# Experts chosen from a table of pairwise comparisons, and another order of the work around the last tile

## The reference: what is computed

```
h   = rmsnorm(x) * g1;   q,k,v,o,i,f,u = h @ w_in
hm  = mLSTM(q, k, v, i, f)  per head, normed, * sigmoid(o)      # running state C, n, m
x1  = x + [hm | multi-scale trailing means of u @ pool_w] @ w_out
h2  = rmsnorm(x1) * g2
group  = top-1 of 4 groups by softmax(h2 @ w_rg + b_rg)
expert = top-2 of the 4 experts of that group by softmax(h2 @ w_re + b_re)
y   = rmsnorm(x1 + sum over the 2 experts of share * (silu(h2 @ w_gate[e]) * (h2 @ w_up[e])) @ w_down[e]) * g_f
```

## Time and profile before

| what | value |
|---|---|
| median of 3 runs | 938.84 us |
| lowest and highest run | 938.76, 940.09 us |
| profiled execution, span from first to last instruction | 939.7 us |
| mean granted TensorE clock | 0.976 |
| PE busy, share of the span | 880.8 us, 94% |
| DVE, POOL, ACT busy | 431.1, 374.6, 154.5 us |

### The profile page before, as it was taken

One profiled execution on the slowest core, in us unless ns is written; L12 is line 12 of the kernel. 1 busy time (PEld: TensorE's weight loads), 2 busy tenths in 40 slices (PEclk: granted clock), 3 DMA queues, 4 the chain that ended last, 5 costly groups with the idle time before them and its releaser, 6 DMA issues.

```text
span 939.7 us, 16689 instructions
## 1 busy us (share of the span) xinstructions
PE 880.8 (94%) x6339; PEld 755.1 (80%) x6339; DVE 431.1 (46%) x1166; ACT 154.5 (16%) x456; POOL 374.6 (40%) x576
## 2 busy tenths in 40 slices
PE   5989999999999999999989799999999999999960
PEld 3974987869588695886945699999999999999920
DVE  3144474645646456463557843333333333333264
ACT  2031212121311213111131210000000000000071
POOL 4040031210302103021150258767767776777524
PEclk9989999999999999999999899999999999999985
DMA  9930203030110301003027389999999999999883
GB/s 328 280 151 1 68 1 80 12 79 1 28 52 1 79 1 34 25 1 57 1 62 291 71 294 299 327 352 335 360 346 333 327 322 326 315 319 314 248 305 115
DMA packets 90039, 163.15 MB, mean 174 GB/s; under 512 B 48887, under 2 KB 59027, under 8 KB 81770
## 3 DMA queue, kind: packets, MB, share of 16 engines
q1 hardware_dynamic: 70062, 136.43, 41.5%
q0 software_dynamic: 17728, 25.28, 11.2%
q10 hardware_dynamic: 2188, 0.59, 0.3%
HBM read 139.83 MB, written 25.87 MB: 176 GB/s over the span
## 4 chain that ended last, share of the span: by engine, by line
PE 51%; DMA 16%; issue 11%; POOL 11%; DVE 9%; ACT 1%; POOLq 1%; DVEq 0%; SPq 0%; ACTq 0%
PE bank L1527 48%; DMA z_d<-wout,win 12%; POOL z_d L599 7%; DVE wout L1443 2%; POOL wout L551 2%; PE bank L1532 1%; DVE wout L1436 1%; DVE win L1482 1%; DMA wout<-h_d,idt 1%; DMA h2T<-z_d 1%; DVE win L1407 1%; PE bank L1732 0%; DMA xbuf<-in_x_prompt 0%; POOL pad L595 0%; PE bank L1645 0%
## 5 line engine op out<-in xcount | busy, mean ns | idle before, releaser
L1527 PE MATMUL bank<-wout,win 128*128 128x150 f32 (+3 forms) x2048 | 246.3, 282 | 1.1 <-DVE wout L1129 1.1
L1527 PEld LDWEIGHTS bank<-wout,win 128*128 128x128 f32 x2048 | 244.7, 190 | 1.2 <-DVE wout L1129 1.2
L1527 PE MATMUL bank<-hT,win 128*128 128x128 f32 (+1 forms) x1536 | 182.9, 279 | 0.0
L1527 PEld LDWEIGHTS bank<-hT,win 128*128 128x128 f32 x1536 | 178.6, 192 | 1.5 <-issue 1.2
L1527 PE MATMUL bank<-win 128*128 128x130 f32 (+5 forms) x1024 | 137.3, 294 | 2.7 <-DVE win L1428 1.4
L599 POOL DMA_INDIRECT z_d<-wout,win x75 | 125.2, 1669 | 27.1 <-issue 26.8
L1527 PEld LDWEIGHTS bank<-win 128*128 128x128 f32 (+2 forms) x1024 | 125.5, 191 | 12.3 <-issue 10.3
L1527 PE MATMUL bank<-win,hT 128*128 128x260 f32 (+3 forms) x512 | 122.2, 417 | 3.0 <-DVE xbuf L1247 1.5
L1527 PE MATMUL bank<-wout,mixT 128*128 128x512 f32 (+1 forms) x384 | 116.8, 487 | 1.8 <-ACT mixT L845 1.7
L1527 PEld LDWEIGHTS bank<-win,hT 128*128 128x128 f32 (+1 forms) x512 | 77.1, 173 | 43.0 <-issue 34.1
L1436 DVE STREAM_TRANSPOSE wout<-bank 128x480 f32<-128x480 f32 (+1 forms) x45 | 25.1, 603 | 156.7 <-DMA z_d<-wout,win 155.2
(11 more groups left out here) (308 smaller groups left out, 812.0 us busy)
## 6 DMA issues: line engine op xcount, KB each, us to landing
win<-in_w_gate SPq DMA_DIRECT2D x32, 1024.0 KB, 6.3
win<-in_w_up SPq DMA_DIRECT2D x32, 1024.0 KB, 9.2
win<-in_w_down SPq DMA_DIRECT2D x32, 1024.0 KB, 10.6
win<-in_w_in SPq DMA_DIRECT2D x4, 2048.0 KB, 20.1
xbuf<-in_x_prompt SPq DMA_DIRECT2D x8, 512.0 KB, 3.8
wout<-in_w_out SPq DMA_DIRECT2D x1, 4096.0 KB, 15.6
z_d<-xbuf SPq DMA_DIRECT2D x32, 128.0 KB
h_d<-xn SPq DMA_DIRECT2D x8, 512.0 KB, 2.7
```

The costliest lines, as they stand in the source:

```text
L1527: return nc.tensor.matmul(out, lhsT, rhs, start=first, stop=last)
```

## The change

Routing: `routing` makes one table of all "a >= b" pairs of the four group values and of the four expert values in each group (5 x 4 x 4 numbers a token), and finds each number's rank by two sums and a subtraction; the group is the number of the highest rank, the experts those of rank one and two. What the first expert alone, the slots and the shares need is split off into `picks_of`, `gaps` and `shares`.

Order: in round 9 the first part of `mix_start` for tile 8 stands ahead of tile 7's norm, with its last product (`decayed`) behind; the state's update, tile 7's logits copy and two of the five `first_turn` transposes stand inside `head_out`, where DVE waits for ACT; ACT's copies of x1 (`picked_rows`) stand behind the decay matrix and the norm. For tile 8, DVE's routing runs straight on in round 9, PE's transposes start with the first half of x1, `seats` (the slots) of tile 7 stands behind tile 8's routing and that of tile 8 behind `first_rows`, and PE's `state_transposes` stands behind `ranks(8)`.

```diff
             def h2_evac(t):
                 R = ROWS[t]
-                after(dve, "h2T_done", t + 1)
                 after(dve, "lo_done", t)
                 for n in range(2):
+                    after(dve, "h2T_done", 2 * t + n + 1)
                     last = v.tensor_tensor(h2T[:, 4 * n:4 * n + 4, 0:R], bank(h2_bank(t, n), P, 4, R),
                                            wide(g2[:, 4 * n:4 * n + 4], [P, 4, R]), ALU.mult)
...
             def routing(t):
...
+                five = rt[0:R, 0:NR].rearrange("p (g e) -> p g e", e=EPG)
+                cubed = [R, EG + 1, EPG, EPG]
+                ge = duel[0:R]
+                ahead, lost, rank = (wins[0:R, c, :].rearrange("p (g e) -> p g e", e=EPG) for c in range(3))
+                goh = rt[0:R, 32:36]
+                link(v.tensor_tensor(ge, five.unsqueeze(3).broadcast_to(cubed), five.unsqueeze(2).broadcast_to(cubed), ALU.is_ge))
+                link(v.tensor_tensor(ge, ge, below[0:R].unsqueeze(1).broadcast_to(cubed), ALU.mult))
+                link(v.tensor_reduce(out=ahead, in_=ge, axis=AX.X, op=ALU.add))
+                link(v.tensor_reduce(out=lost, in_=ge.rearrange("p g a b -> p g b a"), axis=AX.X, op=ALU.add))
+                link(v.tensor_tensor(rank, lost, ahead, ALU.subtract))
+                link(v.tensor_tensor(goh, rank[:, 0], seat[0:R, 0], ALU.is_equal))
+                two = cube_of(R)
+                link(v.tensor_tensor(two, rank[:, 1:], seat[0:R, 1].unsqueeze(1).broadcast_to([R, EG, EPG]), ALU.is_le))
+                v.tensor_tensor(oh[0:R, t, 2, :].rearrange("p (g e) -> p g e", e=EPG), two, wide(goh, [R, EG, EPG]), ALU.mult
+                                ).then_inc(S["route_ready"], 1)
+                dve.wait_ge(S["route_ready"], t + 1)
+            def cube_of(R):
+                return rt[0:R, 64:64 + NE].rearrange("p (g e) -> p g e", e=EPG)
+            def picks_of(t):
+                R = ROWS[t]
+                one = cube_of(R)
+                rank = wins[0:R, 2, :].rearrange("p (g e) -> p g e", e=EPG)
+                link(v.tensor_tensor(one, rank[:, 1:], seat[0:R, 0].unsqueeze(1).broadcast_to([R, EG, EPG]), ALU.is_equal))
+                link(v.tensor_tensor(oh[0:R, t, 0, :].rearrange("p (g e) -> p g e", e=EPG), one, wide(rt[0:R, 32:36], [R, EG, EPG]),
+                                     ALU.mult))
+                link(v.tensor_tensor(oh[0:R, t, 1, :], oh[0:R, t, 2, :], oh[0:R, t, 0, :], ALU.subtract))
+            def gaps(t):
+                R = ROWS[t]
+                diff = rt[0:R, 64:64 + NE]
+                link(v.tensor_reduce(out=rt[0:R, 56:57], in_=rt[0:R, 0:EG], axis=AX.X, op=ALU.max))
+                v.tensor_tensor(rt[0:R, 20:24], rt[0:R, 0:EG], rt[0:R, 56:57].broadcast_to([R, EG]), ALU.subtract)
+                link(v.tensor_tensor(diff, oh[0:R, t, 1, :], oh[0:R, t, 0, :], ALU.subtract))
+                link(v.tensor_tensor(diff, diff, rt[0:R, EG:NR], ALU.mult))
+                v.tensor_reduce(out=rt[0:R, 29:30], in_=diff, axis=AX.X, op=ALU.add).then_inc(S["rexp_in"], 1)
+            def shares(t):
...
+                else:
+                    seats(t)
+            def seats(t):
+                R, place = ROWS[t], rt[0:ROWS[t], 80:96]
+                if t == LAST - 1:
+                    place = kept[0:R]
...
                 v.tensor_tensor(isb[0:R, :, 0:DH], nsb[0:R, :, 0:DH], wide(den, [R, H, DH]), ALU.mult).then_inc(S["hv_ready"], 1)
                 if t == 1:
                     h_evac(3)
+                if t == LAST:
+                    new_state(LAST)
+                    partial_logits(LAST - 1)
+                    first_turn(range(2, 4))
                 after(dve, "hs0", t + 1)
                 r = newton(R, sm[0:R, 16:20], sm[0:R, 24:28], 28, H, 1.0 / DH)
...
                 if i == NT:
                     mix_start(LAST)
+                    norm_x1(LAST - 1)
+                    decayed(LAST)
                     mix_b(LAST)
                     h2_evac(LAST - 1)
-                    first_turn()
+                    first_turn(range(0, 2))
                     numerators(LAST)
-                    partial_logits(LAST - 1)
                     head_out(LAST)
                     logits(LAST - 1)
                     routing(LAST - 1)
+                    picks_of(LAST - 1)
+                    gaps(LAST - 1)
+                    first_turn(range(4, NP))
                     first_scale()
+                    shares(LAST - 1)
                     residual(LAST)
                     places(LAST - 1)
                     h2_evac(LAST)
-                    norm_x1(LAST)
-                    continue
+                    dve.wait_ge(pick_ready, 1)
+                    rms_x1(LAST)
+                    partial_logits(LAST)
+                    logits(LAST)
+                    routing(LAST)
+                    picks_of(LAST)
+                    seats(LAST - 1)
+                    places(LAST)
+                    gaps(LAST)
+                    scale_x1(LAST)
+                    first_rows()
+                    shares(LAST)
+                    seats(LAST)
+                    break
...
-                after(pe, "x1_ready", 2 * t + 2)
+                after(pe, "x1_ready", 2 * t + (1 if t == LAST else 2))
                 after(pe, "hT_ready", min(t + 3, NT))
-                if t == LAST - 1:
-                    after(pe, "x1_ready", 2 * t + 2)
-                else:
+                if t != LAST - 1:
                     after(pe, "mixb_ready", t + 1)
                     after(pe, "state_ready", t + 1)
-                transposed(h2_bank(t, 0), xbuf[0:R, t % 4, 0:512], R, None)
+                transposed(h2_bank(t, 0), xbuf[0:R, t % 4, 0:512], R, "h2T_done")
+                after(pe, "x1_ready", 2 * t + 2)
                 transposed(h2_bank(t, 1), xbuf[0:R, t % 4, 512:1024], R, "h2T_done")
...
                 if i == NT + 1:
                     first_picks(LAST - 1)
-                    state_transposes()
                 if 2 <= i:
                     ranks(i - 2)
                 if i == NT + 1:
+                    state_transposes()
                     first_picks(LAST)
```

More of the change, by code:

```diff
@@ L169, in hymba_step @@
         slots = sb("slots", [P, 2, NT], I32)
+        below = sb("below", [P, EPG, EPG])
+        seat = sb("seat", [P, 2, EPG])
+        duel = sb("duel", [P, (EG + 1) * EPG * EPG])[:, :].rearrange("p (g a b) -> p g a b", g=EG + 1, a=EPG)
+        wins = sb("wins", [P, 3, (EG + 1) * EPG])
+        kept = sb("kept", [P, NE])
         RS = sorted(set(r for r, _ in SLOTS))
@@ L417, in _ @@
                     after(sp, "x1_stored", 16 * NQ * (t + 1))
-                    after(sp, "h2T_done", t + 1)
+                    after(sp, "h2T_done", 2 * (t + 1))
                     load_x(t + 4)
@@ L1064, in logits @@
                 dve.wait_ge(S["lo_read"], t + 1)
[L1066 to L1072, removed]
@@ L1085, in routing @@
[L1085 to L1090, removed]
@@ L1104, in first_picks @@
             def first_picks(t):
-                i, place = t - PICKED[0], rt[:, 80:81]
+                i, place = t - PICKED[0], (kept if t == LAST - 1 else rt[:, 80:96])[:, 0:1]
                 link(v.scalar_tensor_tensor(out=rt[:, 128 + i:129 + i], in0=oh[:, t, 2, 0:1], scalar=-NEAR, in1=place,
@@ L1110, in first_picks, with first_turn @@
                                 ).then_inc(pick_ready, 1)
-            def first_turn():
-                for c in range(NP):
+            def first_turn(pieces):
+                for c in pieces:
                     dve.wait_ge(first[c], 16)
@@ L1134, in places @@
                 after(dve, "rank_done", t + 1)
-                place = rt[0:R, 80:96]
+                place = kept[0:R] if t == LAST - 1 else rt[0:R, 80:96]
                 link(v.tensor_tensor(place, B[7][0:R, 0:NE], cnt[0:R, :], ALU.add))
@@ L1254, in norm_x1, with rms_x1, scale_x1 @@
             def norm_x1(t):
+                rms_x1(t)
+                scale_x1(t)
+            def rms_x1(t):
                 R = ROWS[t]
                 after(dve, "rs20", t + 1)
-                r = newton(R, sm[0:R, 8:9], sm[0:R, 10:11], 11, 1, 1.0 / D)
+                newton(R, sm[0:R, 8:9], sm[0:R, 10:11], 11, 1, 1.0 / D)
+            def scale_x1(t):
+                R, r = ROWS[t], sm[0:ROWS[t], 11:12]
                 after(dve, "h2_stored", 16 * t)
@@ L1278, in _ @@
                 p0 += count
+            link(v.tensor_tensor(below[:, :, :], iof[:, 0:EPG].unsqueeze(2).broadcast_to([P, EPG, EPG]),
+                                 iof[:, 0:EPG].unsqueeze(1).broadcast_to([P, EPG, EPG]), ALU.is_lt))
+            for n, c in enumerate((EPG - 1, EPG - 2)):
+                link(v.tensor_scalar(seat[:, n, :], iof[:, 0:EPG], float(-c), None, ALU.add))
             for n in range(NG):
@@ L1319, in _ @@
                     routing(i - 2)
+                    picks_of(i - 2)
+                    gaps(i - 2)
+                    shares(i - 2)
                     places(i - 2)
```

(4 more changed lines are left out.)

24 lines of the change are left out of this document (13 added, 11 removed).

## The result

The changed kernel takes 941.89 us (median of 20 runs, 940.59 to 944.72) against 940.02 us before (20 runs, 937.78 to 943.26): ratio 1.0024, 95% interval 1.0015 to 1.0033. It is slower, by about 0.2%. The forecast was 935.6 us with a range of 932.5 to 939.0, so both the size and the sign were wrong.

The account below looks back on a forecast made before the run. PE was taken to bound the blocks, with an add loop started by POOL nearly as tight. Block 1 gains 6.2 + 1.31, 7.5 us, but only POOL's 3.2 reaches the end: 938.84 - 3.2 = 935.6, range 932.5 to 939.0.

Parts of the forecast that it names:

- (i) to (iii): Tile 8 up to its logits: mixer gains 3.2 us, heads 1.3, x1 to logits 1.75; together 6.2.
- (iv): Tile 8's routing and picks: 1.9 us instead of 4.4, PE's 1.31 us wait goes, block 1 at 526.75.
- (v): Tile 8's shares and slots behind the first rows on DVE: slots at 528.3, POOL's chain gains only 3.2 us.
- (vi): Block 2: rows scaled at 554.1, PE waits 2.7 us, starts 4.7 earlier; the end comes 3.2 earlier.
- my own case: Whole kernel: 935.6 us, from 933.0 to 937.3; chance 0.51.
- the 1.5 us of stalls: PE's block at 796: pays the 1.5 us between block 2's gain of 4.7 and the add loop's 3.2.
- My second rival: Ahead of block 2: PE's new wait also lowers its clock, costing 1.7 us or twice that; 936.1; chance 0.12.
- The 22.6 us loop: Expert blocks: results, product with the shares, five add DMAs and landing, every 22.6 us, nearly as tight as PE.
- a change of this period: Expert blocks: the prediction counted itself wrong if the period of 22.6 changes.
- The slower rival: Tile 8's slots wait for the first rows, so POOL's scatter starts later; 940.1 us; chance 0.13.
- The third rival: Tile 8's picks run at the slow clock: 2.1 us more before block 1 and the slots; 937.7; chance 0.16.

Follow-up runs that it names:

- order_only: The changed kernel with the old routing in the new order; 944.06 us, ratio 1.0047.
- two_loads: The changed kernel with block 1's and block 2's numbers loaded back to back into two buffers; 934.12 us, ratio 0.9933.
- slots_first: The changed kernel with tile 8's shares and slots ahead of x1's scaling and the first rows on DVE; 933.45 us, ratio 0.9933.
- hold_ids: The changed kernel with SP holding block 2's first half of weights until block 2's numbers have landed; 936.60 us, ratio 0.9984.
- hold_half: The changed kernel with SP holding block 2's first weights until its numbers landed, the second half until its rows landed; 933.34 us, ratio 0.9934.
- table_only: The kernel before with the new table routing, in the old order; 939.74 us, ratio 1.0000.
- keep_clock_8: The changed kernel with 8 identity products on PE between block 1 and block 2; 939.71 us, ratio 1.0002.
- keep_clock: The changed kernel with 16 identity products on PE between block 1 and block 2; 943.44 us, ratio 1.0043.

## Why the prediction was wrong

**(i) to (iii), right.** First output product 496.30 (forecast 496.7), second 504.99 (505.2), logits 516.84 (tile 7's picks were forecast at 516.7 and start at 516.65). The state product is at 1.06 us; a wait of 1.05 for POOL's mask took a little of it.

**(iv), right in its work, a size off.** From the end of the logits to route_ready it is 2.0 us (forecast 1.9). But tile 7's picks took 2.29 us instead of 4.35: the low stretch of the earlier trace rows was gone in this execution. In the new order that is in part luck: the picks took 2.29 us in order_only too, but 3.64 in two_loads and 3.66 in slots_first (in two_loads block 1 came 0.4 us later from the q k product for it). I had kept the 4.35. With PE done sooner, the wait that I had said would go stayed, at 0.98 us of 1.31, and one of 0.18 came with it; block 1 came at 525.39 instead of 526.75.

**(v), a size off.** The slot cast ends at 526.83, forecast 528.3: a gain of 4.65 instead of 3.2, mostly from the same picks.

**(vi), the step that failed.** I moved the rows of block 2 by the gain of the slots, "557.27 - 3.2 = 554.1". This takes everything on POOL between scatter and rows as fixed in length. It isn't: the number load lost 3.9 us and the gather 1.7, the rows were ready at 558.51, and the wait was 8.4 instead of 2.7. For SP I had checked block 1's weights but not block 2's, which hang on PE's half of block 1 and so moved by 8.9 us past a chain that moved by 4.3. In the trace of before both were there: number load at 539.53, weights at 542.79, a distance of 3.3 us against a difference in gains that I had put at 4.3 myself (7.5 less 3.2). With my own numbers the order of the two would have flipped. hold_ids, hold_half, two_loads show it by mending it from either side. Against my sum, block 2 came 4.4 us later (558.56, forecast 554.2), the clock that my own case held at nothing added 1.9, and the 1.5 us of stalls did not come: 4.8 of the 5.1 us between the forecast gain of 3.2 and the measured loss of 1.9.

**The clock.** My second rival had the mechanism (a cost of 1.7 us, measured 1.9), with a wait three times too short beside it. The Trainium skill, page "TensorE: Matmul & The Clock Gate", section "What's actually happening", has half rate as the state that only activity lifts; 18.38 us after the idle wait and 16.5 after identity products agree.

**The 22.6 us loop** was no bound in the changed kernel, where the ten products with the shares from 589.82 to 804.37 come every 21.5 us, nor in table_only, where at the old order the stalls of the earlier trace rows do not occur at all. Why it took 22.6 in the long execution that I read stays open. I had named a change of this period as a sign that I am wrong, and it came. It isn't far from a bound: PE waits for DVE once in a later block of keep_clock_8 (0.90 us), slots_first (0.70) and hold_half (0.17). In the changed kernel nothing of the late block 2 is taken up later, and the sum is plain: block 1 8.5 us earlier from the q k product (36.96 against 45.49), block 2 8.6 us more behind it (33.17 against 24.61), 1.9 for the clock: 1.9 us slower, as the medians say. The two profiled executions hide this: before's, the long one, had 2.15 us more than table_only's 357.62 in its blocks, and the changed one 1.0 more behind the last product group. That last 1.0 isn't explained; it varies by as much between runs of the experiments (46.0 to 47.5 us).

**The slower rival** had the right victim, POOL's chain, and the wrong place: I let it be decided by the slots, which came early. That its 1.3 us of loss lies near the measured 1.9 is chance. The third rival's low clock in tile 8's picks is in order_only (3.45 us), not in the changed kernel (2.28).

## What to carry over

When one chain moves up, list every DMA whose issue hangs on it, and see which other chain's DMAs it now passes; here a chain that ends in a small load and a gather had no length of its own while megabytes were in flight. The longer transfer can be held for the smaller one with a single wait on its queue, or the small one issued earlier; both together turned 0.2% slower into 1% faster here. And before rows are read, see by its time whether the profiled execution is a usual one. An estimate that shifts a chain as a block should name each DMA in it and what else is in flight at the new time.

## What the runs showed of the hardware

A load of 5 KB from POOL's queue took 2.3 to 2.4 us in five kernels, and 6.2 to 6.6 us in four with 2 MB issued from SP's queue 0.9 to 1.6 us ahead of it (the changed kernel, order_only, keep_clock and keep_clock_8). The five gathers of block 2's rows took 7.9 to 10.3 us to the turn in the five kernels where the second 2 MB came 7.2 us or more after their start, and 11.6 to 12.6 in the six where these came at most 4.9 us after it. The Trainium skill, page "DMA: Bandwidth & Descriptors", section "Issuing engines are not separate DMA queues", says that DMAs started by the scalar, sync or gpsimd engine run on the same 16 DMA engines and interleave. These rows agree and add the price.

Gate and up products of 16.5 us at the full clock took 18.26, 18.26, 18.38 and 18.93 us after waits of 2.95 (two_loads), 4.79 (hold_ids), 8.40 (the changed kernel) and 9.22 us (order_only), and 19.32 in block 1 of slots_first after one of 3.19; each of these five has a stretch at a granted clock of 0.50. After waits of 1.57 (hold_half) and 1.66 us (keep_clock_8, behind the identity products) they took 16.59.
